# Attention: which engine splits the next group's queries and keys, and when GpSimd applies their factors

## The reference, cut to what matters

```python
s_s = jnp.einsum('bqgrd,bgqnld->bgrqnl', qb, gk).reshape(b, g, r, NSA_QBLOCK, nl)
p_s = masked_softmax(s_s - slopes * dist_s, dist_s >= 0)     # selected keys
p_w = masked_softmax(s_w - slopes * dist_w, valid_w)         # window keys
p_c = masked_softmax(s_c - slopes * dist_c, dist_c >= 0)     # 32 compressed keys
o = gb[..., 0:1] * o_c + gb[..., 1:2] * o_s + gb[..., 2:3] * o_w
```

## Time and profile before

| | |
|---|---|
| median of 3 runs | 2598.99 us (2593.07 to 2599.32) |
| profiled execution, its own time | 2594.21 us |
| span of its trace | 2592.4 us |
| PE busy | 2486.8 us, 96% of the span |
| POOL, DVE, ACT busy | 1225.9, 887.9, 812.2 us |
| attention stage, first to last exponential | 662.87 to 882.95 us |

### The profile page before, as it was taken

The page is one execution under the profiler, slowest core; times in us unless marked ns, Lnnn a source line. Parts: engine busy times, 40 slices in busy tenths (PEclk is TensorE's granted clock), DMA queues, the critical chain, the costliest instruction groups (busy, mean ns, idle before and its releaser), DMA issues.

```text
span 2592.4 us, 33230 instructions
## 1 busy us (share of the span) xinstructions
PE 2486.8 (96%) x11685; PEld 2029.3 (78%) x11685; DVE 887.9 (34%) x1352; ACT 812.2 (31%) x1546; POOL 1225.9 (47%) x958
## 2 busy tenths in 40 slices
PE   5989999999788999979999999999999999999999
PEld 3777777887688887758888888888888888888887
DVE  3746323157676678771102020202010202020112
ACT  4324223232666622233222222222222222222221
POOL 3654333436577544434444444444444444444443
PEclk8889999999899999989999999999999999999999
DMA  6753222366211277742332333332333333333333
GB/s 273 251 186 102 72 66 92 114 236 204 68 50 58 85 255 261 259 147 90 98 95 92 97 92 94 97 97 89 97 95 92 96 97 90 96 97 92 94 97 114
DMA packets 86227, 316.03 MB, mean 122 GB/s; under 512 B 9584, under 2 KB 10240, under 8 KB 84736
## 3 DMA queue, kind: packets, MB, share of 16 engines
q1 hardware_dynamic: 84240, 303.31, 36.2%
q10 hardware_dynamic: 1904, 11.62, 1.2%
HBM read 310.69 MB, written 4.19 MB: 121 GB/s over the span
## 4 chain that ended last, share of the span: by engine, by line
PE 60%; issue 7%; POOL 5%; DVE 0%; ACT 0%; POOLq 0%; DVEq 0%; ACTq 0%
PE ps L482 55%; POOL wlo L375 4%; PE ps L858 2%; PE ps L847 1%; PE ps L815 1%; PE ps L816 1%; POOL qn L415 0%; PE ps L801 0%; POOL kn L420 0%; PE ps L839 0%; POOL pmod L438 0%; POOL modw L437 0%; POOL oacc L448 0%; POOL q_tok L449 0%; PE ps L967 0%
## 5 line engine op out<-in xcount | busy, mean ns | idle before, releaser
L375 POOL TENSOR_TENSOR wlo<-raw,whi 128x512 fp32r<-128x512 f32 x696 | 927.4, 1334 | 1155.8 <-ACT whi L985 905.9
L985 ACT ACTIVATE whi<-raw 128x512 fp32r<-128x512 f32 x620 | 390.5, 632 | 1298.2 <-PE ps L482 1154.8
L482 PE MATMUL ps<-hfH,whi 128*128 128x512 f32 x1408 | 557.7, 396 | 17.4 <-DVE hfL L1755 13.0
L482 PE MATMUL ps<-hfH,wlo 128*128 128x512 f32 x1408 | 553.4, 393 | 0.0
L482 PE MATMUL ps<-hfL,whi 128*128 128x512 f32 x1408 | 548.1, 389 | 0.0
L482 PEld LDWEIGHTS ps<-hfH,whi 128*128 128x128 f32 x1408 | 265.5, 189 | 72.2 <-issue 13.8
L482 PEld LDWEIGHTS ps<-hfH,wlo 128*128 128x128 f32 x1408 | 265.1, 188 | 62.2
L482 PEld LDWEIGHTS ps<-hfL,whi 128*128 128x128 f32 x1408 | 265.3, 188 | 58.6
L1782 DVE SCALAR_TENSOR_TENSOR x1T<-ps,modc,x1T 128x512 f32<-128x512 f32 x176 | 132.2, 751 | 454.3 <-PE ps L482 454.3
L482 PE MATMUL ps<-huH,whi 128*128 128x512 f32 x704 | 279.1, 397 | 0.5 <-DVE huL L1766 0.5
L482 PE MATMUL ps<-huH,wlo 128*128 128x512 f32 x704 | 279.1, 396 | 0.0
(11 more groups left out here) (277 smaller groups left out, 3066.4 us busy)
## 6 DMA issues: line engine op xcount, KB each, us to landing
raw<-in_wstream SPq DMA_DIRECT2D x370, 512.0 KB, 3.6
modw<-in_mstream SPq DMA_DIRECT2D x160, 512.0 KB, 4.6
modx<-in_mstream SPq DMA_DIRECT2D x32, 512.0 KB, 6.4
xT<-in_xt SPq DMA_DIRECT2D x4, 1024.0 KB, 8.0
w1s<-in_w ACTq DMA_DIRECT2D x2, 2048.0 KB, 8.7
x1T<-in_xt ACTq DMA_DIRECT2D x4, 1024.0 KB, 8.3
out_y<-x1T SPq DMA_DIRECT2D x16, 256.0 KB, 2.0
cmpb<-in_cmp_tab ACTq DMA_DIRECT2D x1, 1024.0 KB, 4.9
```

Source lines behind the costliest of these rows:

```text
L375: nc.gpsimd.tensor_tensor(wlo[:, s, :], raw[:, r, :], whi[:, s, :].bitcast(F32), ALU.subtract).then_inc(unit_ready, 1)
L482: ins = nc.tensor.matmul(acc, lhs, rhs, start=first and n == 0, stop=last and n == 2)
L985: A(whi[:, k % SPLIT, :], raw[:, k % 8, :], ACT.Copy).then_inc(unit_hi, 1)
```

## The change

ACT no longer writes the high part. It copies the transposed bank as it is to one of two SBUF buffers (`stg`, 128x512 fp32 each), and that frees the bank (`n_raw`). DVE makes both parts from the buffer, five units after the transposes: a copy into the high part, then the subtraction, both with all operands in SBUF. ACT waits before it writes a buffer until the parts of two steps ago are made. On DVE `cmp_soft` moves from the tile's unit 0 to 2, `cmp_sum` from 3 to 5; on ACT the exponential of the compressed scores goes behind `save_pt`, and the copy of its transpose one unit ahead; `cmp_values` on PE one unit ahead. On POOL the gains of groups 2 and 3 start in its tiles 3 and 7, ahead of where they were, the scaling of the later queries moves from tile 3 to 2, and the 48 rows are spread unevenly, none in tiles 3, 7 and 15.

```diff
+        POOL_ROWS = (3, 5, 2, 0, 3, 5, 4, 0, 3, 5, 4, 2, 4, 5, 3, 0)
...
-                if tile == 3:
+                if tile == 2:
                     pool.wait_ge(rq_ready, 1)
...
-                if tile in (4, 8):
-                    gains(tile // 4 + 1)
-                for n in range(3 * tile, 3 * tile + 3):
+                if tile in (3, 7):
+                    gains(tile // 4 + 2)
+                for n in range(row_at, row_at + POOL_ROWS[tile]):
                     mod_row(n)
...
-                    pe.wait_ge(pt_saved if kind == "unit" else n_lo, i + 1)
+                    pe.wait_ge(pt_saved if kind == "unit" else n_raw, i + 1)
...
-                if n % 8 == 3 and tile:
+                if n % 8 == 2 and tile:
                     cmp_values(tile - 1)
...
-            def prep_high(g, step):
-                act.wait_ge(n_tr, 6 * g + step + 1)
...
+            def prep_save(g, step):
+                k = 6 * g + step
+                act.wait_ge(n_tr, k + 1)
+                if k == 1:
+                    act.wait_ge(mod_read, 13)
+                if k >= 2:
+                    act.wait_ge(n_lo, k - 1)
+                A(stg[k % 2][:, :], ps[:, prep_bank(g, step), :], ACT.Copy).then_inc(n_raw, 1)
...
-            def prep_low(g, step):
...
+            def prep_parts(g, step):
+
+                k = 6 * g + step
+                dve.wait_ge(n_raw, k + 1)
+                if step == 0 and g >= 2:
+                    dve.wait_ge(s_psum, 32 * (g - 1))
+                    dve.wait_ge(cs_psum, T * (g - 1))
+                raw_k = stg[k % 2]
+                high = kA[g % 2][:, step, :] if step < 2 else qs[g % 2][:, step - 2, :]
+                own(V.tensor_copy(high, raw_k[:, :]))
                 if step < 2:
-                    V.tensor_tensor(kB[g % 2][0:64, step, :], ps[0:64, bank, :],
+                    V.tensor_tensor(kB[g % 2][0:64, step, :], raw_k[0:64, :],
                                     kA[g % 2][0:64, step, :].bitcast(F32), ALU.subtract).then_inc(n_lo, 1)
...
-                if n % 8 == 0 and tile:
+                if 0 <= n - 5 < NU - 32 and (n - 5) % 32 in PREP_AT:
+                    prep_parts((n - 5) // 32 + 1, PREP_AT.index((n - 5) % 32))
+                if n % 8 == 2 and tile:
                     cmp_soft(tile - 1)
-                if n % 8 == 3 and tile:
+                if n % 8 == 5 and tile:
                     cmp_sum(tile - 1)
```

More of the change, by code:

```diff
@@ L187, in layer_kernel @@
         oacc = at("oacc", [P, 3, R * DH])
+        place[0] = abase + 2 * KD * S * 4
+        stg = [at("stg0", [P, S]), at("stg1", [P, S], F32, lg_base)]
         mixH = at("mixH", [P, KD, S], F32R, abase)
@@ L228, in layer_kernel @@
         qk_var, qk_std, qk_norm = (sem(n) for n in ("qk_var", "qk_std", "qk_norm"))
-        n_qk, n_tr, n_hi, n_lo = sem("n_qk"), sem("n_tr"), sem("n_hi"), sem("n_lo")
+        n_qk, n_tr, n_raw, n_lo = sem("n_qk"), sem("n_tr"), sem("n_raw"), sem("n_lo")
         kc_hi, kc_lo, k_zeroed, rq_ready, pool_own = (sem(n) for n in (
@@ L457, in _ @@
             pool.wait_ge(mod_read, 13)
+            row_at = 0
             for tile in range(T * G):
-                if tile == 3:
+                if tile == 2:
                     pool.wait_ge(rq_ready, 1)
@@ L463, in _ @@
                     pool.wait_ge(qk_norm, 3)
-                if tile in (4, 8):
-                    gains(tile // 4 + 1)
-                for n in range(3 * tile, 3 * tile + 3):
+                if tile in (3, 7):
+                    gains(tile // 4 + 2)
+                for n in range(row_at, row_at + POOL_ROWS[tile]):
                     mod_row(n)
+                row_at += POOL_ROWS[tile]
                 add_branches(tile)
@@ L1200, in _ @@
             for step in range(6):
-                prep_high(0, step)
+                prep_save(0, step)
             A(kcA[:, :], kcT[:, :], ACT.Copy).then_inc(kc_hi, 1)
@@ L1207, in _ @@
                     exps(n + 1)
+                if n < NU:
+                    save_pt(n)
                 if n % 8 == 0 and tile:
@@ L1210, in _ @@
                     A(pc[:, :], sc[:, :], ACT.Exp, scale=-1.0).then_inc(cp_ready, 1)
-                if n < NU:
-                    save_pt(n)
-                if n % 8 == 2 and tile:
+                if n % 8 == 1 and tile:
                     act.wait_ge(cpt_psum, tile)
@@ L1216, in _ @@
                 if n // 32 + 1 < G and m in PREP_AT:
-                    prep_high(n // 32 + 1, PREP_AT.index(m))
+                    prep_save(n // 32 + 1, PREP_AT.index(m))
                 if n == 16:
@@ L1610, in invert_queries @@
                 V.tensor_scalar(rq[:, 1, :], rq[:, 1, :], -DH ** -0.5, None, ALU.mult).then_inc(rq_ready, 1)
-            def prep_low(g, step):
-                bank = prep_bank(g, step)
-                dve.wait_ge(n_hi, 6 * g + step + 1)
+            def prep_parts(g, step):
[7 more added lines that the diff above has]
+                own(V.tensor_copy(high, raw_k[:, :]))
                 if step < 2:
-                    V.tensor_tensor(kB[g % 2][0:64, step, :], ps[0:64, bank, :],
+                    V.tensor_tensor(kB[g % 2][0:64, step, :], raw_k[0:64, :],
                                     kA[g % 2][0:64, step, :].bitcast(F32), ALU.subtract).then_inc(n_lo, 1)
@@ L1620, in prep_low @@
                     low = qs[g % 2][64:128, step - 2, :]
-                    V.tensor_tensor(low, ps[64:128, bank, :], low.bitcast(F32), ALU.subtract).then_inc(n_lo, 1)
+                    V.tensor_tensor(low, raw_k[64:128, :], low.bitcast(F32), ALU.subtract).then_inc(n_lo, 1)
             def bias(g, r):
@@ L1668, in _ @@
             for step in range(6):
-                prep_low(0, step)
+                prep_parts(0, step)
             V.memset(mc[:, :], 0.0).then_inc(k_zeroed, 1)
@@ L1703, in _ @@
                         bias(n // 32 + 1, r - 1 + b)
-                if n // 32 + 1 < G and m - 2 in PREP_AT:
-                    prep_low(n // 32 + 1, PREP_AT.index(m - 2))
                 if n in (10, 13):
```

## The result

The changed kernel takes 2604.7 us in the median (16 runs, 2601.69 to 2606.7) against 2599.2 us before (16 runs, 2593.07 to 2607.23): ratio 1.0017, 95% interval 1.0011 to 1.0023. It is slower, by 5.5 us. That is within the 0.3% that the forecast called no change and within its range, but on the other side of 1 than the forecast of 2598.

A forecast was written before the change was run, and what follows sets the result against it. TensorE, busy 96% of the span, bounds the kernel, so only its waits or slow clock give time back. Sum -16.3 + 6.5 - 2 - 2 + 12.8 = -1.0 us on 2594.2; forecast 2598 us, range 2584 to 2611.

The forecast's parts named there:

- Gains one tile earlier: Groups 1 and 2: both TensorE waits for POOL's gains go, and the slow clock behind them; 16.3 us removable.
- Before the first unit: Start: VectorE's six low parts take turns with POOL and end 14 us late, first scores wait; +12.8 us.
- turns from the first: Start: from 656.55, VectorE's 12 instructions have POOL's next 10 between them, 11.1 us in all.
- The rule on the two read ports: VectorE copies in SBUF: single-source fp32 does two elements per cycle; gives start +12.8 us, without it +7.5.
- The first rival, one port: Copies into fp32r take one port: start +7.5, group ends +3.5, 2590 us; chance 0.15.
- the second, that waits don't add up: VectorE's next instruction may slip in before POOL's: start +2.6 to +5, ends near 0, 2583 us; chance 0.10.
- The parts in the groups: VectorE gets +1.7 us per step, 10 us per group; TensorE loses +6.5 us (0 to 13) at group ends.
- ACT's copy to a buffer: Bank free earlier, compressed branch and parts later: slack for VectorE, not TensorE time, except 2 us gained in group 0.
- The last rival, VectorE as the bound of the groups: prep_parts ahead of reduce_scores: groups 1 and 2 about 55.5 us each, group 0 costs 3; +9.3, 2608 us; chance 0.23.
- its own signs: Wrong if start is not late, groups 1 and 2 take under 50 or over 55 us, or holes drop the clock.
- The end: Without mod_row in tile 15, VectorE's last small instructions don't wait for POOL; -2 us (0 to -3.4).
- The base: Sum set on the profiled execution's 2594.2 us; the median of the runs lies 4.8 us above it.

The follow-up runs named there:

- POOL's part alone: Kernel before with only the POOL lines: gains of groups 2 and 3 in tiles 3 and 7, scaling in tile 2, uneven rows; 2586.0 us, ratio 0.9944.
- the last kernel: Kernel before plus POOL's lines and compressed-branch moves, its ACT/TensorE consumers one unit later, old parts from the bank, POOL held back at start; 2570.57 us, ratio 0.9884.
- the wait of one line: Changed kernel with POOL starting gains of group 1 only after VectorE's parts, bias tables and compressed keys' low part of group 0; 2594.61 us, ratio 0.9978.
- the last two kernels: POOL held back and compressed branch one unit later, on the changed kernel (2587.8 us) and on the kernel with the old parts from the bank (2570.57 us).
- fifth run: Changed kernel with group 0 prepared in the old way and the compressed exponential, its transpose and values one unit later; 2591.83 us, ratio 0.9959.

## Why the forecast was right in its range and wrong in its sign

**Gains one tile earlier: -16.3 us.** Right. POOL's part alone gave 14.3 us in groups 1 and 2 and 13.6 us in the median; in the last kernel these groups reach 48.6 and 47.3 us.

**Before the first unit: +12.8 us.** Right in size (+12.7) and in its cause: the wait of one line took the start back to 13.3 us. The picture of turns from the first was wrong, and that the number still came so near is partly luck. In the forecast eleven of the twelve instructions had a POOL instruction in front of them and one ran alone; measured, five had (the first of them seven) and seven ran alone.

**The rule on the two read ports.** A copy of 512 columns into fp32r takes 0.42 us alone, against 0.28 us for the 256 columns of the earlier trace rows and 0.69 us for a subtraction of 512 columns, and it waits for POOL (up to 8.31 us). The Trainium skill (VectorE: DVE Perf Modes, section "Mode 2×_2P — use both read ports for one tensor") gives two elements per cycle for a single source in SBUF; the trace agrees with that rate for fp32r too. The first rival, one port, falls, and at the start so does the second, that waits don't add up.

**The parts in the groups.** The cost on VectorE was right: the 18 steps outside the start took about 44 us together, 2.5 us each, where the forecast had 0.7 + 1.7 us. In TensorE's time they were priced too low: 12.3 us over the four groups, shown by the last two kernels, where the forecast had 6.5 for the group ends. That is within its bounds of 0 to 13.

**The step that failed** is "*ACT's copy to a buffer*", where the moves of the compressed branch were called slack for VectorE, "not time for TensorE", and costed at nothing beyond a gain of 2 us. `cmp_soft` moved two units later on VectorE while its consumers on ACT and TensorE kept their units or moved one ahead, so once per tile ACT's in-order queue stands until VectorE has gone two units further. With the old parts that cost next to nothing (1.8 us of TensorE's waits). The same forecast called VectorE full, and with VectorE full and its instructions stretched by POOL, ACT stood 21.5 us and TensorE 8.3 us: 11.4 us in the groups and 10.3 us in the median, given back by one unit of distance (8.6 and 6.8 us once POOL is held back at the start). With that unit alone, the groups win 16.4 us over before; with POOL held back as well they win 11.8, the number of the forecast, but from two larger terms: 24.1 us from everything except the parts (the last kernel against before), less 12.3 for the parts. Beside this step a term was mis-sized, the 6.5 us of the parts.

**The last rival, VectorE as the bound of the groups.** Its numbers came close: groups 1 and 2 took 54.3 and 57.5 us where it had about 55.5 each, and the profiled difference was +10.0 us where it had +9.3. Part of that is luck, since group 0 won 1.6 us where it had a loss of 3. Its path, the units' minima that come late for ACT and for the scores, is not the main one in the changed kernel: TensorE waits 1.6 us there, and 8.3 us for the compressed exponential. It comes forward once the order is repaired (5.7 us). By its own signs, a group above 55 us and a clock below 1.00, the forecast was wrong.

**The end: -2 us.** It was -0.4. The last `mod_row` ended at 890.3, 0.8 us ahead of the last exponential, not before 875 (about 883 on this trace's scale). VectorE's three stretched small instructions behind it did fall from 0.56, 0.46 and 0.82 us to 0.17 each. But `combine` of the last tile then waited 1.11 us for TensorE's values, so TensorE's wait for the last `add_branches` only went from 3.4 to 2.9 us.

**The base.** The forecast set its sum against a profile 4.8 us faster than the median and did not ask why it was faster. The two lengths of the old start, 12.1 and 17.5 us, would explain that, and the kernel before with POOL held back (6.0 us faster in the median) fits it. Then the changed kernel, with 24.8 us in both traces that have its start, loses 12.7 us against the short start but only about 7.3 against the long one: hence 5.5 us between the medians, and 10.0 us between the profiles. It also means that the forecast stayed within its range with some luck: it had about 5.5 us too much at the start, by the medians, and expected 6.8 us more gain in the groups than came. Why the groups took 3.9 us more when the start was shorter (fifth run) stays open.

## What to carry to other kernels

Where GpSimd has a long queue of its own beside VectorE, an operand moved from PSUM to SBUF can change a VectorE instruction from one that does not wait for GpSimd (the subtraction from the bank took 0.67 to 0.70 us in all 24 steps) into one that waits through many of its instructions (0.68 to 4.0 us from the buffer); price it with the rows where that already happens, and look first at places where nothing else can run. When a producer is moved to a later place in one in-order queue, check at each consumer which independent instruction stands behind the wait: here one unit of distance was worth 7 to 10 us. Before a sum is set against a profile, look at the spread of the runs for a wait that comes in two lengths.

## What the runs showed of the hardware beyond that

VectorE's blocked instruction does not always get its turn when the running GpSimd instruction ends. With GpSimd instructions queued without a wait between them, one copy waited through seven (8.31 us) and one bias table through six (4.37 us, the four 8.13 us), while in the traces of two other kernels, alike at that place, the four took 3.22 and 3.24 us in turns; with nothing beside them they took 2.05. From the start of VectorE's instruction to that of GpSimd's next one it was 0.3 us in both cases (658.54 and 658.83 in turns; 659.89 and 660.17 passed over), so the traces do not tell what decides it.
